# A two-block transformer kernel on one core: GpSimd makes the high weights of three compression units in place of ScalarE

## What is computed

```
def compress(kv, pos, w1, w2):
    blocks = kv[:, idx] + pos          # 15 blocks of 32 tokens, stride 16
    return gelu(blocks @ w1) @ w2      # w1: 2048 x 256, w2: 256 x 64

proj = h @ w_in                        # second projection stage
k_cmp, v_cmp = compress(kc, ..k), compress(vc, ..v)
y_a = sliding-window attention with sinks (8 heads)
y_b = gate0 * compressed + gate1 * selected + gate2 * window attention
```

## Time and profile before

| | |
|---|---|
| Time, median of 3 runs | 863.73 us (863.32 to 864.41) |
| Profiled execution, its own time | 862.67 us |
| Span of the profiled execution | 860.9 us, mean granted clock 0.996 |
| TensorE (PE) busy | 846.5 us, 98% |
| VectorE (DVE) busy | 642.6 us, 75% |
| ScalarE (ACT) busy | 445.4 us, 52% |
| GpSimd (POOL) busy | 73.0 us, 8% |
| 56 copies into `w_hi` of line 462 on ScalarE | 106.4 us, 1910 ns each |

### The profile page before, as it was taken

The page is one execution under the profiler, slowest core; times in us unless marked ns, Lnnn a source line. Parts: engine busy times, 40 slices in busy tenths (PEclk is TensorE's granted clock), DMA queues, the critical chain, the costliest instruction groups (busy, mean ns, idle before and its releaser), DMA issues.

```text
span 860.9 us, 14044 instructions
## 1 busy us (share of the span) xinstructions
PE 846.5 (98%) x5449; PEld 747.2 (87%) x5449; DVE 642.6 (75%) x812; ACT 445.4 (52%) x567; POOL 73.0 (8%) x64
## 2 busy tenths in 40 slices
PE   8999999999999999999999999999999999999995
PEld 6888888889998888888888989889998988888894
DVE  5786765767867686775776877787766798998997
ACT  6455445445333644444444555576435655665663
POOL 1100000004230200000002401200003000000000
PEclk9999999999999999999999999999999999999998
DMA  8875555456743477665466664645545456466441
GB/s 256 306 245 193 193 197 196 165 176 212 229 148 121 132 249 257 207 226 200 152 199 158 162 179 116 185 124 155 180 147 196 147 182 209 146 207 223 154 171 49
DMA packets 119234, 158.11 MB, mean 184 GB/s; under 512 B 4572, under 2 KB 104332, under 8 KB 119068
## 3 DMA queue, kind: packets, MB, share of 16 engines
q1 hardware_dynamic: 116460, 150.93, 54.5%
q0 software_dynamic: 1488, 5.34, 1.8%
q10 hardware_dynamic: 1248, 1.32, 0.5%
HBM read 154.79 MB, written 1.07 MB: 181 GB/s over the span
## 4 chain that ended last, share of the span: by engine, by line
PE 96%; DVE 2%; DMA 1%; issue 0%; ACT 0%; ACTq 0%; DVEq 0%
PE wk L1651 26%; PE acc L1750 25%; PE wk L1620 23%; PE wk L1659 14%; PE wk L2058 1%; PE acc L2028 1%; PE acc L2040 1%; PE acc L1667 1%; DMA x<-in_x 1%; PE wk L2110 0%; PE acc L1767 0%; PE wk L2112 0%; PE acc L1620 0%; DVE x L1569 0%; DVE w_lo L944 0%
## 5 line engine op out<-in xcount | busy, mean ns | idle before, releaser
L1651 PE MATMUL wk<-xhl,w_hi 128*128 128x512 f32 x992 | 239.4, 391 | 0.0
L961 DVE TENSOR_TENSOR w_lo<-raw,w_hi 128x2048 fp32r<-128x2048 f32 x83 | 189.9, 2288 | 64.0 <-ACT w_hi L469 62.8
L1651 PEld LDWEIGHTS wk<-xhl,w_hi 128*128 128x128 f32 x992 | 182.9, 188 | 35.8
L1620 PE MATMUL wk<-xhl,w_hi 128*128 128x256 f32 x896 | 162.8, 287 | 0.1
L469 ACT ACTIVATE w_hi<-raw 128x2048 fp32r<-128x2048 f32 x83 | 158.0, 1903 | 0.0
L1750 PE MATMUL acc<-w_hi,hhl 128*128 128x512 f32 x480 | 153.2, 390 | 0.6 <-issue 0.6
L462 ACT ACTIVATE w_hi<-raw 128x2048 fp32r<-128x2048 f32 x56 | 106.4, 1910 | 68.4 <-PE wk L1620 51.7
L1620 PEld LDWEIGHTS wk<-xhl,w_hi 128*128 128x128 f32 x896 | 137.3, 191 | 2.1 <-issue 0.7
L1659 PEld LDWEIGHTS wk<-xhl,w_lo 128*128 128x128 f32 x992 | 129.4, 191 | 6.3
L944 DVE TENSOR_TENSOR w_lo<-raw,w_hi 128x2048 fp32r<-128x2048 f32 x49 | 114.4, 2337 | 26.8 <-ACT w_hi L462 26.4
L1659 PE MATMUL wk<-xhl,w_lo 128*128 128x256 f32 x992 | 131.1, 282 | 0.0
(11 more groups left out here) (263 smaller groups left out, 943.4 us busy)
## 6 DMA issues: line engine op xcount, KB each, us to landing
raw<-in_ffn_w SPq DMA_DIRECT2D x65, 1024.0 KB, 5.2
raw<-in_w_in SPq DMA_DIRECT2D x26, 1024.0 KB, 6.6
raw<-in_w_ffn_in SPq DMA_DIRECT2D x22, 1024.0 KB, 5.0
raw<-in_w_ffn_out SPq DMA_DIRECT2D x11, 1024.0 KB, 4.8
raw<-in_w_out SPq DMA_DIRECT2D x8, 1024.0 KB, 4.8
arena<-bias_scratch POOLq DMA_DIRECT2D x4, 512.0 KB, 6.1
raw<-in_cmp_w_k SPq DMA_DIRECT2D x2, 1024.0 KB, 5.4
raw<-in_cmp_w_v SPq DMA_DIRECT2D x2, 1024.0 KB, 6.9
```

The lines of the kernel that those rows point to most:

```text
L961: nc.vector.tensor_tensor(w_lo[:, s], raw[:, s], w_hi[:, s].bitcast(F32), ALU.subtract) \
L1620: mm = nc.tensor.matmul(dst, w, v, start=start and n == 0, stop=stop and n == len(pairs) - 1, skip_group_check=True)
L1651: mm = nc.tensor.matmul(bank, wh[:, c, cols], xhl[:, c].rearrange("p n t -> p (n t)"), start=c == 0, stop=False, skip_group_check=True)
```

## The change

For m = 11, 13 and 15 the copy `raw` to `w_hi` leaves ScalarE's list and goes into GpSimd's, behind the three DMAs of line 921. ScalarE gets one new wait ahead of its own `hi` of units 12, 14 and 16, so that `hi_done` still counts units in order. GpSimd's copy has the waits of `hi`, and one more for the same order.

```
@@ ScalarE, in the loop over m
-                    if half == 0:
+                    if half == 0 and m + 2 not in CW[1:]:
+                        if m + 1 in CW[1:]:
+                            act.wait_ge(hi_done, U_IN2 + m + 2)
                         hi(U_IN2 + m + 2)
@@ GpSimd
             for c0, name in ((0, "cmp_w2_k_2"), (HD, "cmp_w2_k_2"), (2 * HD, "cmp_w2_v_2")):
                 nc.gpsimd.dma_start(cmp_w2[:, :, c0:c0 + HD], w_cols(a[name][0])).then_inc(cw2_in, 16)
+            for m in CW[1:]:
+                u = U_IN2 + m
+                pool.wait_ge(raw_in[u % SLOTS], raw_count(u))
+                pool.wait_ge(unit_done, u - 2)
+                pool.wait_ge(hi_done, u)
+                nc.gpsimd.tensor_copy(w_hi[:, u % SLOTS], raw[:, u % SLOTS]).then_inc(hi_done, 1)
             lo_back(U_FFN3, 4)
```

## The result

| | before | after |
|---|---|---|
| Time, median of 6 runs each | 863.34 us (862.85 to 864.41) | 866.83 us (866.15 to 867.71) |
| Ratio | | 1.0041, 95% interval 1.0029 to 1.0053 |
| Profiled execution: own time, span | 862.67, 860.9 us | 866.15, 864.4 us |
| ScalarE busy, GpSimd busy | 445.4, 73.0 us | 440.6, 78.7 us |

The change costs 3.5 us; 2.7 were forecast. The profiled executions stand 3.48 us apart.

The account below looks back on a forecast made before the run. TensorE was taken to bound the kernel, busy 98.65 of 100 us in the stage. A 3.5 us stall less a 0.8 us gain made +2.7 us on 863.73, so 866.4 us, range 864.2 to 869.2.

Parts of the forecast that it names:

- The place and the chain: GpSimd's copy of unit 11 starts behind three DMAs at 548.55; VectorE's low part, step 10's logits, TensorE's step 11 scores wait.
- The length of the copy: Unit 11's 2048-column copy on GpSimd was taken as 2.0 us, with a range up to 3.1.
- The lower bound: GpSimd copy length from the small copy's 0.39 us plus MEMSET's 0.84 ns per further column: 1.9 us.
- The hole: TensorE idle between transposes and scores of step 11, waiting for step 10's logits: cost 3.5 us.
- The clock: Rival: TensorE's clock falls in the step 11 hole, costing 1.8 us more, 868.2 us; chance 0.11.
- The gain: Unit 13's copy off ScalarE removes TensorE's wait at step 14's values for the line 636 copy: 0.8 us.
- the bound of 1.35 us of idle time: TensorE is busy 98.65 of 100 us between 500 and 600 us; more than 1.35 us can't be won there.
- hi(13) and hi(15): High-part copies of units 13 and 15 on GpSimd: cost 0; unit 13's held until unit 12's low part ends on VectorE.
- No recovery: Nothing later in the program waits for a fixed time, so TensorE doesn't recover the loss.
- The sum: Stall of 3.5 us less gain of 0.8 us: +2.7 us, giving 866.4 us.
- the base of 863.73: Median of the runs shown for the kernel before, to which 2.7 us were added for 866.4 us.
- The rival in which the hole closes: Key DMAs land earlier, releasing GpSimd's queue; no stall at step 11, only the 0.8 us gain: 862.9 us; chance 0.12.

Follow-up runs that it names:

- e2: Changed kernel with unit 11's GpSimd copy moved ahead of the wait for the key DMAs and the three DMAs: 861.33 us, 0.9983 of the kernel before.
- e3: Changed kernel with unit 11's GpSimd copy behind the key DMA wait but ahead of the three DMAs: 863.07 us, 0.9999 of the kernel before.
- e7: Changed kernel with unit 11's copy between the second and third of GpSimd's three DMAs: 865.65 us, 1.0033 of the kernel before.
- e8: Changed kernel with a memset of 1024 columns on GpSimd ahead of unit 11's copy: 867.60 us, 1.0056 of the kernel before.
- e9: The changed kernel again, unaltered, measured beside the version with the filled hole: 866.89 us.
- e10: Changed kernel with 13 unused products of zeros on TensorE between transposes and scores of step 11, measured beside the repeated changed kernel: 865.53 us.
- e1: Kernel before with only units 13 and 15 copied on GpSimd, unit 11 on ScalarE: 862.03 us, 0.9989 of the kernel before.
- e6: Kernel before, all copies on ScalarE, its unit 11 copy waiting for a GpSimd memset behind the three DMAs: 867.81 us, 1.0058.
- e5: Kernel before with only unit 11 copied on GpSimd at the change's place, units 13 and 15 on ScalarE: 866.51 us, 1.0044.
- e4: Changed kernel with 13 unused products of zeros on TensorE between transposes and scores of step 11: 865.62 us, 1.0028 of the kernel before.

## Why the prediction was right, step by step

- **The place and the chain: right.** GpSimd's release, the end of its DMA issues (forecast 548.53, in the trace 548.46), the order in which lo(11), the logits behind it and the scores of step 11 wait are as written, and e2, e3, e7 and e8 remove, shorten or lengthen the hole by moving this one start.
- **The length of the copy: 2.0 forecast, 1.89 measured.** The lower bound was the better end. By the Trainium skill (GPSIMD Engine Reference, section "Elementwise — side-by-side cycle accounting") I had estimated 1.8 or 3.1 us; the trace's 1.89 us agrees with the first.
- **The hole: +3.5 forecast, +3.12 measured in the first profile** (+3.36 in e9's, +3.41 in e10's). In the first, 0.1 of the difference is the copy, 0.2 is that TensorE came 0.14 later and GpSimd's copy started 0.05 earlier than in the working, and 0.1 is that the scores started 0.06 us behind the end of the logits (553.32), not 0.2.
- **The clock: wrong.** It stood in the sum with nothing and among the rivals with a chance of 0.11 and a price of 1.8 us. The prediction named its fall as a sign of being wrong, and it fell. It cost 1.50 us in the first profile and 2.46 in e9's, and 1.36 net between the medians of e9 and e10. I argued from the one fall of the trace, 3.7 us after the last product, that a hole of 3.5 was just too short. That was one sample taken as a limit. The Trainium skill (TensorE: Matmul & The Clock Gate, section "Why this matters for your kernels") advises against idle gaps between bursts of products. The runs agree for the holes of 2.3 us and more; the one of 1.03 us in e3 cost no clock.
- **The gain: 0.8 forecast, 1.30 measured (0.92 + 0.38).** The wait of 0.82 went as said. The second part, the wait of 0.22 ahead of the transposes of step 14, went with the clock's fall, which makes TensorE later still: in e1 0.21 of it remains, and in e10, with the hole but the clock held, it is 0.39. With the clock held the gain is 0.89 - 0.16 = 0.7 in e10's trace, close to the forecast. Both waits also show that idle time is less than what a wait costs: 0.82 us of idle time were 0.92 from row to row, and 0.22 were 0.38. So the bound of 1.35 us of idle time was not quite a bound on the time that can be won.
- **hi(13) and hi(15): 0, right.** That hi(13) would be stretched by lo(12) was right for e1 (3.19 us) and e10 (3.38 us), and wrong for the changed kernel (1.90): at the lower clock unit 10 ended so late that hi(13) began at 559.38, 0.1 us before lo(12) was over.
- **No recovery: right,** by the ledger's stretch from step 14 to the last instruction.

The sum was +2.7; the ledger has +3.12 + 1.50 - 1.30 = +3.3, and 0.14 that TensorE was already late at step 10. The hole was put 0.4 too long and the gain 0.5 too small, both errors against the change, and together they hid 0.9 of the clock's 1.5 in the first profile. That the forecast time of 866.4 us came within 0.4 of the measured 866.83 is in part luck: the base of 863.73 was 0.4 above the median of all six runs of the kernel before, while the difference was forecast at 2.7 and measured at 3.5. The mechanism that was added up is right, as e10's +2.7 shows; the changed kernel is 0.8 above it in the first measurement and 1.4 beside e10, because of the clock. The rival in which the hole closes did not occur. e2, which takes hi(11) out of its place in the queue, shows that it was priced too low: it gained 1.7 us by the medians and 1.3 in the trace, where the rival had 0.8.

## What to carry to other kernels

Moving work to an idle engine moves it into that engine's queue: look first for what stands ahead of the new place, and when that was released in the trace, then for what is queued behind the instruction that waits. Here the engine was 8% busy and the copy as fast as on ScalarE, yet the wait for transfers and the three DMA starts in front of it made all the difference between 3.5 us slower and 1.7 us faster. And price a new hole in TensorE's work twice, once for its length and once for the clock behind it. One profile shows one execution: see first where its time lies among the others of the same kernel.

## What was not expected of the hardware

- The granted clock fell in holes of 2.3, 2.7, 3.05, 3.3 and 4.1 us and in one of 1.81 + 1.29, and held in one of 1.03. In the profiled executions the scores of step 11 were then 5.72 (changed), 6.68 (e9), 6.68 (e6), 6.90 (e5), 7.15 (e7) and 6.70 us (e8) from the transposes of step 12, against 4.22: the fall cost 1.5 to 2.9 us, and the shortest single hole had the dearest fall. It differs between executions of one kernel too: the changed kernel's six have a mean clock of 0.993 to 0.995 and times of 866.15 to 867.71, the lowest clocks with the longest times.
- A cast from float32 to fp32r of 128x2048 takes 1895 ns on GpSimd and 1911 on ScalarE (means of 3 and of 53 in the changed kernel). Where it began on GpSimd under a VectorE subtraction of two SBUF inputs it took 3.19 to 3.38 us (e1, e3, e4, e10).
- The same key DMAs were landed between 0.40 us (e5) and 1.09 us (e4) after the transposes of step 10, though all work before them was the same. A start that hangs on such a landing carries that scatter. In the trace of the kernel before it was 0.98 us.
